# A float32r kernel of four blocks: where the streamed activations lie within 256 bytes

## What is computed

```python
for l in range(2):                                    # first block
    h = h + 0.5 * swiglu(rmsnorm(h, g[l, 0]), gate[l, 0], up[l, 0], down[l, 0])   # 1024 -> 2816 -> 1024
    h = h + mixer(rmsnorm(h, g[l, 1]), w_in[l], ...)
    h = h + 0.5 * swiglu(rmsnorm(h, g[l, 2]), gate[l, 1], up[l, 1], down[l, 1])
for l in range(2):                                    # second block
    z = (rms_norm(x, ln1_g[l]) * (1.0 + sc1) + sh1) @ w_in[l]
    ...
    x = x + g1 * (merged @ w_out[l])
    h2 = rms_norm(x, ln2_g[l]) * (1.0 + sc2) + sh2
    x = x + g2 * (jnp.square(jax.nn.relu(h2 @ w_ff1[l])) @ w_ff2[l])              # 1024 -> 4096 -> 1024
```

## The kernel before

| what TensorE streams | columns | place of high / low part, bytes |
|---|---|---|
| `xn` and `h` in ffn(0,0), ffn(0,1), ffn(1,0), `xn` in mix 0 | 272 | 0 / 128 |
| `xn` in mix 1, most units | 256 | 64 / 192 |
| `xn` and `h` in ffn(1,1) | 256 | 0 / 128 in even k tiles, 128 / 0 in odd ones |
| `xn` in ln1 and ff, both layers | 258 | 0 / 128 |
| `f` in ff, both layers | 256 | 0 / 128 in even k tiles, 128 / 0 in odd ones |

## Time and profile before

### The profile page before, as it was taken

The page is one execution under the profiler, slowest core; times in us unless marked ns, Lnnn a source line. Parts: engine busy times, 40 slices in busy tenths (PEclk is TensorE's granted clock), DMA queues, the critical chain, the costliest instruction groups (busy, mean ns, idle before and its releaser), DMA issues.

```text
span 1856.3 us, 36263 instructions
## 1 busy us (share of the span) xinstructions
PE 1842.2 (99%) x15151; PEld 1803.0 (97%) x15151; DVE 1372.6 (74%) x2385; ACT 1040.5 (56%) x1734; POOL 1.3 (0%) x8
## 2 busy tenths in 40 slices
PE   9999999999999999999999999999999999999998
PEld 8999998899999999999899999999999999999998
DVE  6787786577776678668667887798877559788754
ACT  6444565655444545466656445676665457656643
POOL 0000000000000000000000000000000000000000
PEclk9999999999999999999999999999999999999999
DMA  8876333357785577634346787354555554445553
GB/s 281 291 272 247 133 122 111 114 170 257 267 299 185 208 269 289 227 120 137 103 155 230 275 284 283 131 179 157 175 190 182 182 179 169 163 163 194 185 186 114
DMA packets 53123, 365.59 MB, mean 197 GB/s; under 512 B 6652, under 2 KB 9116, under 8 KB 11488
## 3 DMA queue, kind: packets, MB, share of 16 engines
q1 hardware_dynamic: 52960, 363.26, 56.1%
HBM read 362.19 MB, written 1.05 MB: 196 GB/s over the span
## 4 chain that ended last, share of the span: by engine, by line
PE 95%; DVE 3%; ACT 1%; DMA 1%; issue 0%; SPq 0%; DVEq 0%; ACTq 0%
PE bank L503 28%; PE bank L504 28%; PE bank L505 28%; PE bank L560 2%; PE bank L556 1%; PE bank L557 1%; DVE w_lo L1648 1%; PE bank L789 1%; PE bank L774 1%; PE bank L819 0%; PE bank L726 0%; DMA ada_raw<-in_ada_w 0%; PE bank L949 0%; PE bank L964 0%; PE bank L720 0%
## 5 line engine op out<-in xcount | busy, mean ns | idle before, releaser
L503 PE MATMUL bank<-xn_hi,w_hi 128*128 128x272 f32 (+3 forms) x2672 | 771.1, 289 | 1.6 <-DVE w_lo L1648 1.6
L504 PE MATMUL bank<-xn_hi,w_lo 128*128 128x272 f32 (+3 forms) x2672 | 757.8, 284 | 0.0
L505 PE MATMUL bank<-xn_lo,w_hi 128*128 128x272 f32 (+3 forms) x2672 | 757.7, 284 | 0.0
L503 PEld LDWEIGHTS bank<-xn_hi,w_hi 128*128 128x128 f32 (+1 forms) x2672 | 501.8, 188 | 9.3 <-issue 4.4
L504 PEld LDWEIGHTS bank<-xn_hi,w_lo 128*128 128x128 f32 (+1 forms) x2672 | 503.0, 188 | 1.0
L505 PEld LDWEIGHTS bank<-xn_lo,w_hi 128*128 128x128 f32 (+1 forms) x2672 | 501.4, 188 | 0.0
L1108 ACT ACTIVATE w_hi<-raw_a 128x1024 fp32r<-128x1024 f32 (+2 forms) x278 | 303.3, 1091 | 284.3 <-PE bank L505 251.3
L1108 ACT ACTIVATE w_hi<-raw_b 128x1024 fp32r<-128x1024 f32 (+2 forms) x280 | 305.3, 1090 | 272.8 <-PE bank L505 245.0
L1648 DVE TENSOR_TENSOR w_lo<-raw_b,w_hi 128x1024 fp32r<-128x1024 f32 (+2 forms) x280 | 354.1, 1265 | 136.0 <-ACT w_hi L1108 134.8
L1648 DVE TENSOR_TENSOR w_lo<-raw_a,w_hi 128x1024 fp32r<-128x1024 f32 (+2 forms) x278 | 351.6, 1265 | 124.7 <-ACT w_hi L1108 124.3
L503 PE MATMUL bank<-h_hi,w_hi 128*128 128x272 f32 (+1 forms) x704 | 201.4, 286 | 0.3 <-DVE full L1842 0.3
(11 more groups left out here) (349 smaller groups left out, 2634.7 us busy)
## 6 DMA issues: line engine op xcount, KB each, us to landing
raw_b<-in_weights SPq DMA_DIRECT2D x122, 1024.0 KB, 4.8
raw_a<-in_weights SPq DMA_DIRECT2D x121, 1024.0 KB, 4.8
ada_raw<-in_ada_w SPq DMA_DIRECT2D x48, 1024.0 KB, 5.3
raw_a<-in_weights SPq DMA_DIRECT2D x16, 1408.0 KB, 5.9
raw_b<-in_weights SPq DMA_DIRECT2D x16, 1408.0 KB, 5.8
c_rows<-in_c_rows SPq DMA_DIRECT2D x3, 512.0 KB, 6.3
raw_a<-in_weights SPq DMA_DIRECT2D x2, 768.0 KB, 4.2
raw_b<-in_weights SPq DMA_DIRECT2D x2, 768.0 KB, 4.2
```

The source lines that it names most:

```text
L503: pe.matmul(o, wh, xh, start=start, stop=False)
L504: pe.matmul(o, wl, xh, start=False, stop=False)
L505: return pe.matmul(o, wh, xl, start=False, stop=stop)
```

## The change

A table `PLACE` gives each stage a column offset for the high part and one for the low part, and `streams` hands out both tensors from there. The offsets of a pair differ by 32 columns, which takes the low part's own 128 bytes back, so that high and low rows start at the same place within 256 bytes; and the move of odd k tiles is gone from `xn` and `h`. All writers (ScalarE's and VectorE's rounding, the shift columns) and all readers use it. Counting the tensors' own places, the rows now start here:

| stage | columns | place before, high / low | place after, both |
|---|---|---|---|
| ffn(0,0) `xn` | 272 | 0 / 128 | 64 |
| ffn(0,0) `h` | 272 | 0 / 128 | 128 |
| mix 0 `xn` | 272 | 0 / 128 | 128 |
| ffn(0,1) `xn`, and `h` | 272 | 0 / 128 | 192 |
| ffn(1,0) `xn` | 272 | 0 / 128 | 32 |
| ffn(1,0) `h` | 272 | 0 / 128 | 64 |
| mix 1 `xn`, 272 columns (few units) | 272 | 0 / 128 | 160 |
| mix 1 `xn`, 256 columns | 256 | 64 / 192 | 224 |
| ffn(1,1) `xn`, and `h` | 256 | alternating | 128 |
| ln1 of layer 0, of layer 1 | 258 | 0 / 128 | 128, 192 |
| ff of layer 0, of layer 1, `xn` | 258 | 0 / 128 | 64, 96 |

`a`, `b`, `y`, `f` and the small tensors of the second block keep their places and `stream` its rule. The number, the order and the shapes of the instructions are the same on every engine, and so are the waits; only start addresses differ.

```diff
+PLACE = {("ffn", 0, 0): (16, 48), ("mix", 0): (32, 0), ("ffn", 0, 1): (48, 16), ("ffn", 1, 0): (8, 40), ("mix", 1): (40, 8),
+         ("ffn", 1, 1): (32, 0), ("ln1", 0): (32, 0), ("ff", 0): (16, 48), ("ln1", 1): (48, 16), ("ff", 1): (24, 56),
+         ("h", 0, 0): (32, 0), ("h", 0, 1): (48, 16), ("h", 1, 0): (16, 48), ("h", 1, 1): (32, 0)}
+
+
+def streams(c, stage):
+
+    hi, lo = (c.h_hi, c.h_lo) if stage[0] == "h" else (c.xn_hi, c.xn_lo)
+    width = N + 2 if stage[0] in ("ln1", "ff") else T
+    return tuple(x[:, :, at:at + width] for x, at in zip((hi, lo), PLACE[stage]))
...
     def ffn(l, f):
         u, stage, cols = FIRST["gu", l, f], ("ffn", l, f), LIVE[l] if f else TA
-        to = packed(cols)
+        to, (hh, hl) = packed(cols), streams(c, ("h", l, f))
...
-                    tile(u + b, at, to, c.xn_hi, c.xn_lo)
+                    tile(u + b, at, to, *streams(c, stage))
...
-                        m = product(bank[b][:, to], wh[:, s], wl[:, s], stream(c.h_hi, kf, to), stream(c.h_lo, kf, to), kf == 0, kf == KF - 1)
+                        m = product(bank[b][:, to], wh[:, s], wl[:, s], stream(hh, kf, to), stream(hl, kf, to), kf == 0, kf == KF - 1)
...
     def before_norm(stage, kk, gain, cols, to):
 
-        hi = stream(c.xn_hi, kk, to) if stage[0] in ("ffn", "mix") else c.xn_hi[:, kk, to]
+        hi = streams(c, stage)[0][:, kk, to]
...
                     act.wait_ge(*k.at("gated", (l, f, i, j)))
-                    act.activation(stream(c.h_hi, 2 * i + j, to), c.full[:, j, to], ACT.Copy).then_inc(*k.up("x_hi", ("h", l, f, i, j)))
+                    act.activation(streams(c, ("h", l, f))[0][:, 2 * i + j, to], c.full[:, j, to], ACT.Copy).then_inc(*k.up("x_hi", ("h", l, f, i, j)))
...
-                    low(stream(c.h_lo, 2 * i + j, to), c.full[:, j, to], stream(c.h_hi, 2 * i + j, to), ("h", l, f, i, j))
+                    hi, lo = (x[:, 2 * i + j, to] for x in streams(c, ("h", l, f)))
+                    low(lo, c.full[:, j, to], hi, ("h", l, f, i, j))
```

More of the change, by code:

```diff
@@ L574, in leading_units @@
         if stage == ("ffn", 0, 0):
-            first_units(c.xn_hi, c.xn_lo, ("g", *stage))
+            first_units(*streams(c, stage), ("g", *stage))
         else:
-            tiles_as_ready(u, 0, to, c.xn_hi, c.xn_lo, ("g", *stage), norm)
+            tiles_as_ready(u, 0, to, *streams(c, stage), ("g", *stage), norm)
         if stage[0] == "mix":
-            tiles_as_ready(u + 2, 2, to, c.xn_hi, c.xn_lo, stage)
+            tiles_as_ready(u + 2, 2, to, *streams(c, stage), stage)
         else:
@@ L584, in leading_units @@
             for i in (2, 3):
-                tile(u + i, i, to, c.xn_hi, c.xn_lo)
+                tile(u + i, i, to, *streams(c, stage))
     def half_tiles(u, bs, cols, xh, xl, ready=()):
@@ L642, in log_gates @@
         pe.wait_ge(*k.at("x_lo", ("lr", l)))
+        xh, xl = streams(c, ("mix", l))
         for kk in range(KD):
             ks = slice(32 * kk, 32 * kk + 32)
-            m = product(bank[4][0:32, 0:T], c.lr_hi[:, ks], c.lr_lo[:, ks], stream(c.xn_hi, kk, TA), stream(c.xn_lo, kk, TA), kk == 0, kk == KD - 1)
+            m = product(bank[4][0:32, 0:T], c.lr_hi[:, ks], c.lr_lo[:, ks], stream(xh, kk, TA), stream(xl, kk, TA), kk == 0, kk == KD - 1)
         m.then_inc(*k.up("gla_mm", ("lr", l)))
@@ L857, in mixer @@
                 b = VALUE_TILE_BANKS[u - 4]
-                tile(u0 + u, b, TA, c.xn_hi, c.xn_lo)
+                tile(u0 + u, b, TA, *streams(c, stage))
                 free[b] = [("tile_a", ("vT", l, u - 4))]
@@ L862, in mixer @@
             elif u == 13:
-                tile(u0 + u, 1, TA, c.xn_hi, c.xn_lo)
+                tile(u0 + u, 1, TA, *streams(c, stage))
                 free[1] = [("tile_a", ("vbT", l))]
@@ L866, in mixer @@
                 b = 0 if u in (8, 10, 12, 14) else u % 2
-                tile(u0 + u, b, TA if u == 12 else live, c.xn_hi, c.xn_lo)
+                tile(u0 + u, b, TA if u == 12 else live, *streams(c, stage))
                 free[b] = [("tile_v" if 14 <= u < 20 else "tile_a", ("in", l, u))]
@@ L900, in ff @@
                 if i:
-                    tile(u + b, at, TX, c.xn_hi, c.xn_lo)
+                    tile(u + b, at, TX, *streams(c, stage))
                 free[at] = [("tile_v", ("ff1", l, 4 * i + b))]
@@ L1033, in mixer2 @@
                 if at > 3:
-                    tile(u, b, TX, c.xn_hi, c.xn_lo, rows=64 if at == 5 else P)
+                    tile(u, b, TX, *streams(c, stage), rows=64 if at == 5 else P)
                 free[b] = [("tile_v", ("n2", l, at))]
@@ L1138, in normalised @@
         for kk in range(KD):
-            f, hi = c.full[:, kk % 2, 0:to.stop - to.start], stream(c.xn_hi, kk, to)
+            f, hi = c.full[:, kk % 2, 0:to.stop - to.start], streams(c, stage)[0][:, kk, to]
             act.wait_ge(*k.at("scaled", (*stage, kk)))
@@ L1169, in shift_column @@
         for i, part in enumerate((1.0, 0.5)):
-            act.activation(c.xn_hi[:, :, N + i], c.mod_all[:, l, first:first + 8], ACT.Copy, scale=part).then_inc(*k.up("x_hi", ("shift", l, first, i)))
+            act.activation(streams(c, ("ff" if first else "ln1", l))[0][:, :, N + i], c.mod_all[:, l, first:first + 8], ACT.Copy, scale=part).then_inc(*k.up("x_hi", ("shift", l, first, i)))
     def split_piece(q):
@@ L1702, in normalised @@
                 scaled(kk + 1)
-            f, hi, lo = c.full[:, kk % 2, 0:n], stream(c.xn_hi, kk, to), stream(c.xn_lo, kk, to)
+            f, (hi, lo) = c.full[:, kk % 2, 0:n], (x[:, kk, to] for x in streams(c, stage))
             low(lo, f, hi, (*stage, kk))
@@ L1707, in before_norm @@
     def before_norm(stage, kk, gain, cols, to):
-        hi, lo = (stream(xn, kk, to) if stage[0] in ("ffn", "mix") else xn[:, kk, to] for xn in (c.xn_hi, c.xn_lo))
+        hi, lo = (xn[:, kk, to] for xn in streams(c, stage))
         dve.wait_ge(*k.at("x_hi", ("g", *stage, kk)))
@@ L1740, in shift_column @@
     def shift_column(l, first):
+        hi, lo = streams(c, ("ff" if first else "ln1", l))
         for i, part in enumerate((1.0, 0.5)):
             dve.wait_ge(*k.at("x_hi", ("shift", l, first, i)))
-            dve.scalar_tensor_tensor(out=c.xn_lo[:, :, N + i], in0=c.mod_all[:, l, first:first + 8], scalar=part, in1=c.xn_hi[:, :, N + i].bitcast(F32),
+            dve.scalar_tensor_tensor(out=lo[:, :, N + i], in0=c.mod_all[:, l, first:first + 8], scalar=part, in1=hi[:, :, N + i].bitcast(F32),
                                      op0=ALU.mult, op1=ALU.subtract).then_inc(*k.up("x_lo", ("shift", l, first, i)))
```

## The result

The changed kernel takes 1863.69 us (median of 5 runs, 1863.46 to 1864.68) against 1856.61 us for the kernel before in the same comparison: a ratio of 1.004, 95% interval 1.0029 to 1.005. It is slower by 7 us, clear of the 0.2% that can be told, where 1841.6 us and a gain had been forecast.

A forecast was written before the change was run, and what follows sets the result against it. TensorE, busy 99% of 1856.3 us, was taken to be bound by its matmul pace; 7.4 + 6.4 + 0 + 1.2 = 15.0 us off gave a span of 1841.3 and, with 0.3 us, 1841.6 us; range 1825 to 1874.

The forecast's parts named there:

- That only the pace could change: Whole kernel: the change moves no instruction and no wait, so it can only alter the pace of TensorE's matmuls.
- The cover of ScalarE and VectorE: Writers, 56% and 74% busy, stay hidden while TensorE frees weights late, even at a pace 1% faster; nothing in the sum.
- The 0.3 us that the sum adds between span and median: Added to the forecast span of 1841.3 us to give the forecast time of 1841.6 us.
- 272 columns, -7.4 us forecast: 272-column stages, 5712 matmuls: all kinds last 286 ns instead of mean 287.3, 1.3 ns less each.
- its 126.7 ns: Upward bound for 272 columns: mix 1's 120.0 ns from six 256-column matmuls, taken to 272 columns; a loss of 2.3 ns.
- 258 columns, -6.4 us forecast: 258-column stages, 2544 matmuls: a common place other than 0 takes 2.5 ns off the 120.0 ns pace.
- ffn(1,1), 0 forecast: ffn(1,1), 256 columns: giving up alternation for a constant 128 changes nothing, as half the rows were at 128 already.
- the bound of 5.0: Upward bound for ffn(1,1): 5.0 us more if its constant place runs at mix 1's 120.0 ns.
- mix 1: Its 256-column part, 528 matmuls, going from 64 / 192 to 224: 2.2 ns off each, 1.2 us gained.
- The rival with the worse lock: Places relative to the weights choose a slower cycle, as in mix 1: 16.7 us lost, 1873 us; chance 0.30, whole or in part.
- That places change nothing: By the skill's page TensorE has its own read ports and waits on nobody, so 1856.6 us stays; rival "nothing" 0.12.
- The pace by the Trainium skill: Warm pace of columns at 2.4 GHz plus some 2.5 ns: 109.2 ns at 256 columns, where the window shows 116.7.

The follow-up runs named there:

- undo272: Changed kernel with `xn` of ffn(0,0), ffn(0,1), ffn(1,0) and `h` of ffn(0,1), ffn(1,0) back at places 0 / 128; 1857.65 us against 1856.34, ratio 1.0009.
- swapped: Against the changed kernel: 272- and 258-column stages at 128 high / 0 low, ffn(1,1) constant 0 / 128; 1863.57 us, kernel before 1857.37.
- all128: Changed kernel with every stage of the table at place 128, high and low alike; 1852.52 us in one run, kernel before 1859.72.
- w0_x192: Changed kernel with all table stages at place 192 and the weights moved from place 192 to 0; 1856.28 us, kernel before 1857.37.

## Why the prediction was wrong

- **That only the pace could change** held: no instruction or clock moved and no wait came in, the account in paces gives 5.4 of 6.0 us of span, and with the first stage 7.7 against the 7.1 us between the medians. The cover of ScalarE and VectorE held too. (The 0.3 us that the sum adds between span and median join two executions: the profiled one took 1857.56 us, 1.3 more than its span and 1.0 more than the median. That is below what can be told.)
- **272 columns, -7.4 us forecast: the step that failed.** It took the figure of place 128 (286 ns) for 64, 192 and 32, on the ground that only place 0 was known to be dear. By pace, 128 gave 1.1 ns, close to the 1.3 forecast, but only in `h` of ffn(0,0) and in mix 0 (-1.5 us); 192 lost 0.9 and 64 and 32 lost 2.3 ns, +5.0 us, and another 2.3 us in the first stage by its pace. The run undo272, which takes back just these places, is back at the kernel before. The prediction had the better evidence in hand, mix 1 at 64 / 192 and its 126.7 ns for 272 columns, and put it down as a rival.
- **258 columns, -6.4 us forecast**, +2.9 measured: the second step that failed, and nearly as large. Neither did a place other than 0 help (122.2 at 64, 120.0 at 192 and 96), nor was place 0 the dear one: alike at 0 it gives 118.8, the best seen. To blame a matmul's duration on its own place was the error, here and at 272 columns; durations in a cycle of unequal places don't belong to the places one by one, as the run swapped shows.
- **ffn(1,1), 0 forecast**, 1.4 us lost, inside the bound of 5.0; swapped shows that it was the alternation. **mix 1**, -1.2 forecast, about -0.7.
- **`f`, not in the sum at all**, was 1.7 us shorter in the profiled execution. A stage that an edit does not touch can change its pace, and it can do so between two executions of one kernel; so this is no effect that can be put down to the change.
- **The rival with the worse lock** was right in kind, in its price for 64 and 32, and in its rule that it decides when the stages away from 128 lose more than 128 gains. It was too dear for 192 (126.7 for 125.3) and for ffn(1,1) (5.0 for 1.4), hence 1873 for 1864. That its 126.7 ns agree to a tenth is luck: it was a pace at 256 columns, 120.0 from six matmuls, with 16 columns added. At 256 columns place 64 measured 118.7 and 192 measured 120.0, at 272 columns 126.7 and 125.3, so that adding columns gives neither. It should have had the larger chance all the same: it rested on a row, the forecast on the absence of one.
- **That places change nothing**, which the prediction drew from the Trainium skill ("SBUF — State Buffer", section "Who interferes with whom"), did not come true: 123.3 to 126.7 ns for one shape, with nothing but addresses different. The pace by the Trainium skill ("TensorE: Matmul & The Clock Gate", section "Wait — 56ns, not 53.3ns?"), 109.2 ns at 256 columns as an estimate from it, is not reached in any stretch of these runs; the best was 113.3.

## What to carry to other kernels

Where TensorE is full with float32r matmuls, measure the distance between starts, stretch by stretch, and compare it for equal shapes: where streamed rows start relative to the weights was worth 2.7% of it here (123.3 to 126.7 ns). Sweep one place through all stages instead of reasoning from the durations of single kinds, since these only have a meaning as a cycle. And expect a later stage to move from one pace to another with what comes before it, or from one execution to the next; when an untouched stage changes, look at its paces, in more than one execution, before looking for a cause in the edit.

## What the runs showed of the hardware

- The pace of a stretch goes by where the streamed row starts relative to the weights, not by its own place: rows 64 bytes before the weights had the same pace at 128 with weights at 192 and at 192 with weights at 0 (all128 and w0_x192: 327 and 327, 851 and 852, 664 and 664 matmuls in equal windows). Other distances were not tested in this way, nor whether 256 bytes is the period. Steps of 16 bytes count (124.4 ns at 80, 126.7 at 64, 123.4 at 96).
- One layout can have two stable paces: 113.3 and 117.8 ns at 256 columns, place 128; 120.0 and 126.6 at 258 columns, 128/0; 116.7 and 117.8 in `f`, the last pair in two executions of one kernel. An extra matmul of 16 columns moved a stretch from the long to the short one, one of 32 columns moved it back. That it is a phase of entry that chooses is a reading of this; no run measures such a phase.
- The best pace at 256 columns was 113.3 ns, 272 cycles of 2.4 GHz; at 272 columns it was 123.3 ns, 296 cycles, at 258 columns 118.8 ns, 285 cycles. Why 256 columns come within 16 cycles of their number and 272 columns only within 24 is open, and so is what inside TensorE or the memory makes the cycles; it was not tried beyond places and pauses.
